# A two-layer hybrid block: two of layer 1's modulation products moved from its input projections to the start of the layer

## The chip, the cores and the metric

One Trainium2 chip, one core of it. The time is the device time of one execution in microseconds (us); lower is better.

## The reference

256 latent and 256 context tokens of width 1024 in float32 pass two layers. Cut to what matters here:

```python
for l in range(DEPTH):                                    # 2
    mod_l = split(silu(c) @ ada_w[l] + ada_b[l], 6)       # shift, scale, gate; shift, scale, gate
    mod_c = split(silu(c_ctx) @ ada_w[l] + ada_b[l], 6)
    pl = modulate(rms_norm(xl, norm1_g[l]), mod_l[0], mod_l[1]) @ w_in[l]
    pc = modulate(rms_norm(xc, norm1_g[l]), mod_c[0], mod_c[1]) @ w_in[l]
    ml, mc = token_mixing(pl, pc, ...)                    # pooling, two attentions, gated MLP
    xl = xl + mod_l[2] * (ml @ w_out[l])
    hl = modulate(rms_norm(xl, norm2_g[l]), mod_l[3], mod_l[4])
    xl = xl + mod_l[5] * grouped_moe(hl, ...)             # 16 experts, 2 for each token
    ...                                                   # the same for xc in layer 0
return rms_norm(xl, final_g)
```

The modulation (`c @ ada_w[l]`) depends on no token. `ada_w[l]` is 1024 x 6144, 24 MB for each layer.

## The kernel before, in words

The five engines run programs written out by hand, tied by semaphores; the order of instructions on each engine is that of the source.

**Weights in blocks.** Every large weight is loaded in blocks of 256 columns (1 MB; the second block of `w_in` is 160 columns, 0.64 MB) into a ring of six slots `raw`. All loads are issued by one queue, SP, in the order of `ORDER[l]` (line 354 on), and each waits until the block six places ahead of it has left its slot (`free_slot`, line 520; the load itself is line 548). A block of `w_in`, `w_out` or an expert is split on ACT and DVE into a rounded part `w_hi` and a rest `w_lo` (lines 808 and 1803; for experts 1033 and 2068), and TensorE (PE) takes three products for each (lines 1176 to 1178, for one kind of block 1298 to 1300). A block of `ada_w` is not split: PE multiplies it as it is.

**Modulation in quads.** A quad is four blocks of `ada_w`, one of the six vectors of a layer, quads 0 to 5 for layer 0 and 6 to 11 for layer 1. `modulate` (line 1197, the products are line 1205) waits until its four blocks have landed and runs 32 matmuls, four column groups by eight, into one PSUM bank. DVE copies the result to `mod_row` (`take_rows`, line 1824), PE transposes it (`turn`, line 1213), and DVE adds the bias and writes the vector (`take_modulation`, line 1832, with 1839 for the two scale vectors 7 and 10). `AFTER_BLOCK` names the block of `w_in` behind which a quad is computed; quads 6 and 7 of layer 1 are computed in layer 0, quads 9 and 10 in the projections of layer 1 behind its blocks 3 and 5, quads 8 and 11 in the attentions of the two layers (`IN_ATTENTION`). Quad 8 and the four before it are so all ready before layer 1 starts. Quads 9 and 10 are read first in the second half of layer 1.

**Between the layers.** The expert outputs of layer 0 are stored to DRAM. When the stores have landed, POOL gathers each token's two rows back, a 128-token tile at a time, eight gathers of 512 KB (line 773), and then clears a tile (line 672) on which SP's `small_loads` of layer 1 wait (line 560 on: seven small parameters, the last of them `na_bias`, two transfers in pieces of 256 bytes). For each tile ACT scales one row (line 862) and DVE adds the other (line 1890). Then `combine` works in eight units (four tiles by two halves): PE transposes four 128 x 128 pieces (line 1244), DVE adds them, gated, to the stream `x_t` (line 1897), ACT squares the result (line 856), PE sums the squares (line 1256). The eight sums end in a root on ACT, a reciprocal on DVE, and `rows_of` (line 1194) on PE, which spreads it. Then the norm of layer 1 delivers its input piece by piece, and PE starts block 0.

Meanwhile SP has put the first six blocks of layer 1 into the slots of the last experts (`next_layer`), then it sends the small loads, then it goes on with the order. ACT and DVE split blocks 0 and 1 ahead of the norm.

**Projections.** Eight blocks of `w_in` follow each other on PE (`W_COLS`); behind each come small products (`after_block`) and, where named, a quad, whose turn stands in the middle of the next block (`between`). From block 3 on each is split behind the block two before it (`SPLIT_AFTER`).

Of the kernel before, what the change touches and what calls it, by code (L numbers as in the profile page):

```python
# [115 lines left out]
def build(nc, a, out):  # L116
    with ExitStack() as ctx:  # L117
# [129 lines left out]
        assert M.at <= area_at + area_size  # L247

        mod_row = nc.alloc_sbuf_tensor_at("mod_row", [P, 2, BW], F32, offset=sgu_w_at)

        pair_hi = [xg_hi, nc.alloc_sbuf_tensor_at("pair_hi", [P, KC, 2 * SLOTS], F32R, offset=h_at + 2 * KC * T)]
        pair_lo = [xg_lo, nc.alloc_sbuf_tensor_at("pair_lo", [P, KC, 2 * SLOTS], F32R, offset=h_at + 6 * KC * T)]
# [81 lines left out]
        def rounds_before(l):  # L334
            return sum(ROUNDS[:l])
# [9 lines left out]
        W_COLS = [6, 7, 5, 4, 0, 1, 2, 3]  # L345
        W_SLOT = [0, 1, 2, 0, 1, 0, 1, 0]
        OUT_SLOT = [0, 1, 2, 1]
        AFTER_BLOCK = [{2: 2, 3: 3, 4: 4, 5: 5, 6: 6, 7: 7}, {3: 9, 5: 10}]
        IN_ATTENTION = [8, 11]
        SPLIT_AFTER = [{1: (3,)}, {1: (3,), 2: (4,), 3: (5,), 4: (6,), 5: (7,)}]  # L350
        SPLIT_FIRST = [{3: 4, 4: 5, 5: 6, 6: 7}, {}]
        ORDER = []
        for l in range(DEPTH):
            w_in_blocks = [(l, N_ADA + b) for b in range(N_WIN)]
            w_out_blocks = [(l, N_ADA + N_WIN + b) for b in range(N_WOUT)]
            order = quad(0) + quad(1) if l == 0 else []
            for n in range(N_WIN):
                order = order + [w_in_blocks[n]]
                if n in AFTER_BLOCK[l]:
                    order = order + quad(AFTER_BLOCK[l][n])  # L360
            ORDER.append(order + quad(IN_ATTENTION[l]) + w_out_blocks)

# [148 lines left out]
        def combine_units(l):  # L511

            return [(t, half) for t in range(2 * streams(l)) for half in range(2)]
# [659 lines left out]
        def _(pe):  # L1173
# [35 lines left out]
            def turn(q, dst):  # L1209

                pe.wait_ge(m_row, q + 1)
                for c in range(2):
                    ins = pe.transpose(dst[:, BW + c * P:BW + (c + 1) * P], mod_row[:, q % 2, c * P:(c + 1) * P], ident)
                ins.then_inc(m_turn, 1)

            def norm(i, width):

                n = width // P
                if i == 0:
                    for k in range(KC):  # L1220
                        pe.wait_ge(n_sqa if k % 2 == 0 else n_sqd, k // 2 + 1)
                        column_sums(bank[6], nsq[:, k % 4, :], k, n, k == KC - 1).then_inc(n_sum, 1)
                    turn(0, bank[START_BANK[0]])
                if i == 2 * DEPTH:
                    for c in range(KC):
                        pe.wait_ge(n_sqc, DEPTH * KC + c + 1)
                        column_sums(bank[SUM_BANK[i]], nsq_f[:, c % 4, :], c, n, c == KC - 1).then_inc(n_suc, 1)
                pe.wait_ge(n_rstd, i + 1)
                rows_of(bank[7], rstd, n).then_inc(n_bc, 1)
                if i == 0:  # L1230
                    modulate(1, bank[START_BANK[1]])
                    turn(1, bank[START_BANK[1]])

            def combine(l, u):

                units = combine_units(l)
                n = sum(len(combine_units(i)) for i in range(l))
                t, half = units[u]
                pe.wait_ge(q_c, n // 2 + t + 1)
                if u >= 3:  # L1240
                    pe.wait_ge(x_moe, n + u - 2)
                for c in range(4):
                    k = 4 * half + c
                    ins = pe.transpose(bank[4 + u % 3][:, c * P:(c + 1) * P], y_back[:, t, 0, k * P:(k + 1) * P], ident)
                ins.then_inc(q_ct, 1)
                if u >= 2:
                    unit_sums(l, u - 2)
                if u == len(units) - 1:
                    unit_sums(l, u - 1)
                    unit_sums(l, u)  # L1250
# [15 lines left out]
            for l in range(DEPTH):  # L1266
# [3 lines left out]
                if l == 0:  # L1270
                    pe.wait_ge(s_xin, 64)
                    for k in range(KC):
                        if k >= 6:
                            pe.wait_ge((s_xevd, s_xev)[k % 2], 1)
                        for t in range(4):
                            ins = pe.transpose(bank[X_BANK[k]][:, t * P:(t + 1) * P], x_tok[t][:, k * P:(k + 1) * P], ident)
                        ins.then_inc(s_xt, 1)
                    modulate(0, bank[START_BANK[0]])
                else:

                    pe.wait_ge(q_ya, E * rounds_before(l))
                    pe.wait_ge(q_yd, E * rounds_before(l))
                    for u in range(len(combine_units(l - 1))):
                        combine(l - 1, u)
                norm(2 * l, T)


                def by_feature(n, dst, c0, m, width, l=l):
                    s = W_SLOT[n]
                    for k in range(KC):  # L1290
                        ins = product(dst[0:m, 0:width], w_hi[s][:, k, c0:c0 + m], w_lo[s][:, k, c0:c0 + m],
                                      h_hi[:, k, 0:width], h_lo[:, k, 0:width], k == 0, k == KC - 1)
                    return ins
# [72 lines left out]
                for n in range(N_WIN):  # L1366
                    wait_split(l, N_ADA + n)
                    if n >= 2:
                        pe.wait_ge(proj_ea, l * 6 + (1, 2, 3, 4, 4, 5)[n - 2])
                        pe.wait_ge(proj_ed, l * 5 + (1, 2, 2, 2, 3, 3)[n - 2])  # L1370
                    b0 = 2 * (n % 2)

                    def between(n=n):
                        if n - 1 in AFTER_BLOCK[l]:
                            turn(AFTER_BLOCK[l][n - 1], bank[7])

                    if n == 0:
                        s = W_SLOT[0]
                        for k in range(KC):
                            pe.wait_ge(n_lo, l * KC + k + 1)  # L1380
                            for c in range(2):
                                cs = slice(c * P, (c + 1) * P)
                                ins = product(bank[c][:, 0:width], w_hi[s][:, k, cs], w_lo[s][:, k, cs],
                                              h_hi[:, k, 0:width], h_lo[:, k, 0:width], k == 0, k == KC - 1)
                    elif n == 1:
                        by_feature(n, bank[2], 0, P, T)
                        ins = by_feature(n, bank[3], P, 2 * ROPE, T)
                    elif W_COLS[n] in (3, 4, 5):
                        for t in range(4 if W_COLS[n] == 3 else nt):
                            if t == 1:  # L1390
                                between()
                            ins = by_token(n, bank[b0 + t // 2][:, (t % 2) * BW:(t % 2 + 1) * BW], t)
                    else:
                        for c in range(2):
                            if c == 1:
                                between()
                            ins = by_feature(n, bank[b0 + c], c * P, P, T if W_COLS[n] == 2 else width)
                    ins.then_inc(used, 1)
                    if n in AFTER_BLOCK[l]:
                        q = AFTER_BLOCK[l][n]  # L1400
                        if q > min(AFTER_BLOCK[l].values()):
                            pe.wait_ge(s_mod, q)
                        modulate(q, bank[7])
                    after_block(n)
# [383 lines left out]
        def _(dve):  # L1788
# [30 lines left out]
            def take_rows(q, src):  # L1819

                dve.wait_ge(ada_mm, q + 1)
                if q >= 2:
                    dve.wait_ge(m_turn, q - 1)
                dve.tensor_copy(mod_row[:, q % 2, :], src[:, 0:BW]).then_inc(m_row, 1)

            def take_modulation(q, src):

# [74 lines left out]
            for l in range(DEPTH):  # L1902
                ns = streams(l)
                nt, width = 2 * ns, ns * S
                if l == 0:
                    for k in range(0, KC, 2):
                        dve.wait_ge(s_xt, k + 1)
                        dve.tensor_copy(x_t[:, k, :], bank[X_BANK[k]][:, :]).then_inc(s_xevd, 1)
                    dve.wait_ge(s_xev, 4)
                else:  # L1910
                    for r in range(HL - 1):
                        split(l, N_ADA + r)
                    for u in range(len(combine_units(l - 1)) + 1):
                        combine(l - 1, u)
                    dve.wait_ge(x_moe, sum(len(combine_units(n)) for n in range(l)))

                def before_modulation():
# [2 lines left out]
                    take_rows(1, bank[START_BANK[1]])  # L1920
                    take_modulation(1, bank[START_BANK[1]])

                norm(2 * l, T, False, None if l else before_modulation)
                if l == 0:
                    split(0, N_ADA + 1)
                split(l, N_ADA + HL - 1)
# [448 lines left out]
```

## Time and profile before

| | |
|---|---|
| median of 3 runs | 933.02 us (931.19 to 935.28) |
| profiled execution, its own time | 933.12 us |
| its span, first to last instruction | 931.3 us |
| mean granted PE clock | 0.935 |
| PE busy | 841.8 us, 90% |
| DVE busy | 552.3 us, 59% |
| ACT busy | 463.6 us, 50% |
| POOL busy | 78.3 us, 8% |
| DMA | 197.49 MB, 212 GB/s over the span |

Busy is the time in which an engine had an instruction in work, as a share of the span; overlapping matmuls count once. The granted clock is 1.00 at 2.4 GHz and 0.50 at 1.2 GHz. Times in the views are us from the start of the span. A row of the timeline is one instruction or several alike, with start, length, engine and line, what is written from what, and their number; in brackets stands the time for which the engine had nothing to do before, and what ended it. SPq is the queue engine SP, whose rows are DMA issues; "to landing" is the time from an issue to the semaphore that tells its end.

### The profile page before, as it was taken

The page shows a single profiled execution, that of the slowest core. Times are in us where ns is not written, and L with a number is a line of the kernel's source. Part 1 is how long each engine was busy: PE and PEld are TensorE (multiplying, and loading weights), DVE is VectorE, ACT ScalarE, POOL GpSimd, SP SyncE. Part 2 cuts the span into 40 slices and gives each one's busy share as a digit, 9 for nine tenths or more (in the row PEclk, how much of TensorE's full clock was granted, in tenths as well). Part 3 has the DMA queues.
Part 4 walks back from the last instruction along what each step waited for, and adds up shares of the span by engine and source line. Part 5 has one row for each costly group of instructions (what it writes and reads, how often), then busy time and mean ns, then how long its engine had stood idle before and what let it go on. Part 6 is the DMA issues. An engine that isn't in the chain of part 4 may idle for free. (4 is left out here: it accounts for less than half of the span.)

```text
span 931.3 us, 15158 instructions
## 1 busy us (share of the span) xinstructions
PE 841.8 (90%) x6042; PEld 717.3 (77%) x6042; DVE 552.3 (59%) x804; ACT 463.6 (50%) x637; POOL 78.3 (8%) x103
## 2 busy tenths in 40 slices
PE   2899999899998889999999557999999799999986
PEld 2668866766787789999999456887769599999974
DVE  1363312359534878777777465444385678888953
ACT  1363112068523666655665336422384557776734
POOL 0102001600012000000000132001301100000000
PEclk9799999999998599999999856999999799999996
DMA  9795897793021158888888792269163249999901
GB/s 324 239 307 150 279 321 248 227 343 97 29 91 46 42 172 277 291 297 279 292 287 280 252 267 85 79 220 320 40 203 125 72 136 321 346 341 329 349 34 46
DMA packets 165442, 197.49 MB, mean 212 GB/s; under 512 B 11346, under 2 KB 152572, under 8 KB 165372
## 3 DMA queue, kind: packets, MB, share of 16 engines
q1 hardware_dynamic: 160720, 180.70, 60.7%
q10 hardware_dynamic: 3500, 11.64, 3.2%
q0 software_dynamic: 1152, 4.19, 1.4%
q8 instruction: 46, 0.75, 0.3%
q14 instruction: 24, 0.20, 0.1%
HBM read 187.09 MB, written 9.44 MB: 211 GB/s over the span
## 5 line engine op out<-in xcount | busy, mean ns | idle before, releaser
L2068 DVE TENSOR_TENSOR w_lo<-raw,w_hi 128x2048 fp32r<-128x2048 f32 x96 | 219.4, 2290 | 37.6 <-ACT w_hi L1033 37.0
L1033 ACT ACTIVATE w_hi<-raw 128x2048 fp32r<-128x2048 f32 x96 | 183.5, 1913 | 64.8 <-PE bank L1178 55.8
L1176 PE MATMUL bank<-h_hi,w_hi 128*128 128x512 f32 (+2 forms) x288 | 105.4, 366 | 12.0 <-DVE h_lo L1860 10.1
L1176 PE MATMUL bank<-w_hi,xg_hi 128*128 128x256 f32 x384 | 111.1, 289 | 2.3 <-DVE xg_lo L2229 1.7
L1177 PE MATMUL bank<-w_lo,xg_hi 128*128 128x256 f32 x384 | 108.6, 283 | 0.0
L1178 PE MATMUL bank<-w_hi,xg_lo 128*128 128x256 f32 x384 | 108.6, 283 | 0.0
L1177 PE MATMUL bank<-h_lo,w_hi 128*128 128x512 f32 (+2 forms) x288 | 101.6, 353 | 0.0
L1178 PE MATMUL bank<-h_hi,w_lo 128*128 128x512 f32 (+2 forms) x288 | 101.5, 353 | 0.0
L1803 DVE TENSOR_TENSOR w_lo<-raw,w_hi 128x2048 fp32r<-128x2048 f32 (+1 forms) x20 | 45.4, 2277 | 54.1 <-ACT w_hi L808 54.0
L808 ACT ACTIVATE w_hi<-raw 128x2048 fp32r<-128x2048 f32 (+1 forms) x20 | 37.2, 1866 | 76.9 <-PE bank L1178 26.2
L1176 PEld LDWEIGHTS bank<-w_hi,xg_hi 128*128 128x128 f32 x384 | 73.4, 191 | 2.7 <-issue 2.6
L1177 PEld LDWEIGHTS bank<-w_lo,xg_hi 128*128 128x128 f32 x384 | 73.6, 192 | 0.0
L1178 PEld LDWEIGHTS bank<-w_hi,xg_lo 128*128 128x128 f32 x384 | 73.5, 191 | 0.0
L1176 PEld LDWEIGHTS bank<-h_hi,w_hi 128*128 128x128 f32 (+1 forms) x288 | 54.7, 190 | 23.5 <-issue 9.5
L1592 PE MATMUL bank<-onehot,h_tok 128*128 128x256 f32 x512 | 65.1, 286 | 1.3 <-DVE onehot L2074 1.3
L1592 PEld LDWEIGHTS bank<-onehot,h_tok 128*128 128x128 f32 x512 | 64.1, 194 | 2.3 <-ACT h_tok L880 1.7
L1178 PEld LDWEIGHTS bank<-h_hi,w_lo 128*128 128x128 f32 (+1 forms) x288 | 54.8, 190 | 8.2
L1177 PEld LDWEIGHTS bank<-h_lo,w_hi 128*128 128x128 f32 (+1 forms) x288 | 54.9, 191 | 7.7 <-issue 0.2
L1176 PE MATMUL bank<-w_hi,ht_hi 128*128 128x512 f32 x128 | 51.9, 405 | 5.2 <-DVEq L2332 2.6
L1178 PE MATMUL bank<-w_hi,ht_lo 128*128 128x512 f32 x128 | 51.3, 401 | 0.0
L1177 PE MATMUL bank<-w_lo,ht_hi 128*128 128x512 f32 x128 | 51.2, 400 | 0.0
L1205 PE MATMUL bank<-raw,c_pad 128*32 128x256 f32 x768 | 45.4, 390 | 1.3 <-DMA raw<-in_ada_w 1.3
(291 smaller groups left out, 1615.6 us busy)
## 6 DMA issues: line engine op xcount, KB each, us to landing
raw<-in_ada_w SPq DMA_DIRECT2D x48, 1024.0 KB, 10.2
raw<-in_moe_w_gate SPq DMA_DIRECT2D x32, 1024.0 KB, 6.0
raw<-in_moe_w_up SPq DMA_DIRECT2D x32, 1024.0 KB, 6.3
raw<-in_moe_w_down SPq DMA_DIRECT2D x32, 1024.0 KB, 5.0
raw<-in_w_in SPq DMA_DIRECT2D x14, 1024.0 KB, 10.5
raw<-in_w_out SPq DMA_DIRECT2D x8, 1024.0 KB, 9.1
y_rows<-y_sb ACTq DMA_DIRECT2D x16, 512.0 KB, 4.8
na_bias<-in_na_rpb SPq DMA_DIRECT2D x4, 384.0 KB, 8.7
```

The lines of the kernel that those rows point to most:

```text
L808: act.activation(w_hi[slot][:, :, 0:w], raw[n % RAW][:, :, 0:w], ACT.Copy).then_inc(split_hi, 1)
L1033: act.activation(w_hi[slot][:, :, :], raw[q][:, :, :], ACT.Copy).then_inc(split_hi, 1)
L1176: pe.matmul(dst, w_hi_, x_hi_, start=first, stop=False)
L1177: pe.matmul(dst, w_hi_, x_lo_, start=False, stop=False)
L1178: return pe.matmul(dst, w_lo_, x_hi_, start=False, stop=last)
L1205: ins = pe.matmul(dst[32 * g:32 * g + 32, 0:BW], c_pad[:, k, :], raw[raw_index(l, j) % RAW][:, k, :], start=(k == 0), stop=(k == KC - 1))
L1592: ins = pe.matmul(bank[c // 2][:, (c % 2) * 2 * SLOTS:(c % 2 + 1) * 2 * SLOTS], h_tok[part][:, t, c * P:(c + 1) * P], onehot[:, t, :], sta ...
L1803: dve.tensor_tensor(w_lo[slot][:, :, 0:w], raw[n % RAW][:, :, 0:w], w_hi[slot][:, :, 0:w].bitcast(F32), ALU.subtract).then_inc(split_lo, 1)
L2068: dve.tensor_tensor(w_lo[slot][:, :, :], raw[q][:, :, :], w_hi[slot][:, :, :].bitcast(F32), ALU.subtract).then_inc(split_lo, 1)
```

## The change

Quads 9 and 10 leave the projections. Quad 9 is computed on PE between the last expert of layer 0 and `combine`; its copy and its additions on DVE stand behind the two splits and ahead of the gathered tiles. Quad 10 is computed behind unit 3 of `combine`, that is when tiles 0 and 1 are through; its copy stands on DVE behind the last unit, its turn on PE behind the last sum, its additions between the reciprocal and the norm. Both use banks 2 and 3 and a row buffer of their own, `gap_row`, as the place of `mod_row` is taken by a small parameter there. PE's product of block 1, which writes bank 3, now waits for quad 10's additions. In the order of loads, all eight quad blocks stand behind block 1 of `w_in`, so that the six slots filled at the end of layer 0 hold blocks 0 and 1 and quad 9; quad 10, blocks 2 to 7 and quad 11 follow. No product and no load is added or taken away.

```diff
--- before.py
+++ after.py
@@ -247,6 +247,7 @@
         assert M.at <= area_at + area_size
 
         mod_row = nc.alloc_sbuf_tensor_at("mod_row", [P, 2, BW], F32, offset=sgu_w_at)
+        gap_row = nc.alloc_sbuf_tensor_at("gap_row", [P, 2, BW], F32, offset=area_at + 16384)
 
         pair_hi = [xg_hi, nc.alloc_sbuf_tensor_at("pair_hi", [P, KC, 2 * SLOTS], F32R, offset=h_at + 2 * KC * T)]
         pair_lo = [xg_lo, nc.alloc_sbuf_tensor_at("pair_lo", [P, KC, 2 * SLOTS], F32R, offset=h_at + 6 * KC * T)]
@@ -345,8 +346,9 @@
         W_COLS = [6, 7, 5, 4, 0, 1, 2, 3]
         W_SLOT = [0, 1, 2, 0, 1, 0, 1, 0]
         OUT_SLOT = [0, 1, 2, 1]
-        AFTER_BLOCK = [{2: 2, 3: 3, 4: 4, 5: 5, 6: 6, 7: 7}, {3: 9, 5: 10}]
+        AFTER_BLOCK = [{2: 2, 3: 3, 4: 4, 5: 5, 6: 6, 7: 7}, {}]
         IN_ATTENTION = [8, 11]
+        IN_GAP, GAP_BANK = [9, 10], [2, 3]
         SPLIT_AFTER = [{1: (3,)}, {1: (3,), 2: (4,), 3: (5,), 4: (6,), 5: (7,)}]
         SPLIT_FIRST = [{3: 4, 4: 5, 5: 6, 6: 7}, {}]
         ORDER = []
@@ -356,6 +358,8 @@
             order = quad(0) + quad(1) if l == 0 else []
             for n in range(N_WIN):
                 order = order + [w_in_blocks[n]]
+                if l == 1 and n == 1:
+                    order = order + quad(IN_GAP[0]) + quad(IN_GAP[1])
                 if n in AFTER_BLOCK[l]:
                     order = order + quad(AFTER_BLOCK[l][n])
             ORDER.append(order + quad(IN_ATTENTION[l]) + w_out_blocks)
@@ -1209,8 +1213,9 @@
             def turn(q, dst):
 
                 pe.wait_ge(m_row, q + 1)
+                rows = gap_row if q in IN_GAP else mod_row
                 for c in range(2):
-                    ins = pe.transpose(dst[:, BW + c * P:BW + (c + 1) * P], mod_row[:, q % 2, c * P:(c + 1) * P], ident)
+                    ins = pe.transpose(dst[:, BW + c * P:BW + (c + 1) * P], rows[:, q % 2, c * P:(c + 1) * P], ident)
                 ins.then_inc(m_turn, 1)
 
             def norm(i, width):
@@ -1280,8 +1285,13 @@
 
                     pe.wait_ge(q_ya, E * rounds_before(l))
                     pe.wait_ge(q_yd, E * rounds_before(l))
+                    modulate(IN_GAP[0], bank[GAP_BANK[0]])
+                    turn(IN_GAP[0], bank[GAP_BANK[0]])
                     for u in range(len(combine_units(l - 1))):
                         combine(l - 1, u)
+                        if u == 3:
+                            modulate(IN_GAP[1], bank[GAP_BANK[1]])
+                    turn(IN_GAP[1], bank[GAP_BANK[1]])
                 norm(2 * l, T)
 
 
@@ -1383,6 +1393,8 @@
                                 ins = product(bank[c][:, 0:width], w_hi[s][:, k, cs], w_lo[s][:, k, cs],
                                               h_hi[:, k, 0:width], h_lo[:, k, 0:width], k == 0, k == KC - 1)
                     elif n == 1:
+                        if l:
+                            pe.wait_ge(s_mod, IN_GAP[1] + 1)
                         by_feature(n, bank[2], 0, P, T)
                         ins = by_feature(n, bank[3], P, 2 * ROPE, T)
                     elif W_COLS[n] in (3, 4, 5):
@@ -1821,7 +1833,8 @@
                 dve.wait_ge(ada_mm, q + 1)
                 if q >= 2:
                     dve.wait_ge(m_turn, q - 1)
-                dve.tensor_copy(mod_row[:, q % 2, :], src[:, 0:BW]).then_inc(m_row, 1)
+                rows = gap_row if q in IN_GAP else mod_row
+                dve.tensor_copy(rows[:, q % 2, :], src[:, 0:BW]).then_inc(m_row, 1)
 
             def take_modulation(q, src):
 
@@ -1910,8 +1923,11 @@
                 else:
                     for r in range(HL - 1):
                         split(l, N_ADA + r)
+                    take_rows(IN_GAP[0], bank[GAP_BANK[0]])
+                    take_modulation(IN_GAP[0], bank[GAP_BANK[0]])
                     for u in range(len(combine_units(l - 1)) + 1):
                         combine(l - 1, u)
+                    take_rows(IN_GAP[1], bank[GAP_BANK[1]])
                     dve.wait_ge(x_moe, sum(len(combine_units(n)) for n in range(l)))
 
                 def before_modulation():
@@ -1920,7 +1936,10 @@
                     take_rows(1, bank[START_BANK[1]])
                     take_modulation(1, bank[START_BANK[1]])
 
-                norm(2 * l, T, False, None if l else before_modulation)
+                def gap_modulation():
+                    take_modulation(IN_GAP[1], bank[GAP_BANK[1]])
+
+                norm(2 * l, T, False, gap_modulation if l else before_modulation)
                 if l == 0:
                     split(0, N_ADA + 1)
                 split(l, N_ADA + HL - 1)
```

On PE between the layers, before (`y_back` is the gathered tile, `nsq_t` the squares, `rstd` the reciprocal root):

```order
L1244 MATMUL bank<-const,y_back 128x128 x12
L1256 MATMUL bank<-const,nsq_t 128x1 x4
L1244 MATMUL bank<-const,y_back 128x128 x4
...
L1244 MATMUL bank<-const,y_back 128x128 x4
L1256 MATMUL bank<-const,nsq_t 128x1 x12
L1194 MATMUL bank<-const,rstd 128x128 x4
```

and with the change, from behind the last product of quad 9 (`raw` times `c_pad` is a quad's product, 32 such rows; `gap_row` is its copied row):

```order
L1218 MATMUL bank<-const,gap_row 128x128 x2
L1249 MATMUL bank<-const,y_back 128x128 x12
L1261 MATMUL bank<-const,nsq_t 128x1 x4
L1249 MATMUL bank<-const,y_back 128x128 x4
L1261 MATMUL bank<-const,nsq_t 128x1 x4
...
L1249 MATMUL bank<-const,y_back 128x128 x4
L1261 MATMUL bank<-const,nsq_t 128x1 x4
...
L1249 MATMUL bank<-const,y_back 128x128 x4
L1261 MATMUL bank<-const,nsq_t 128x1 x12
L1218 MATMUL bank<-const,gap_row 128x128 x2
L1198 MATMUL bank<-const,rstd 128x128 x4
```

The 32 products of quad 10 stand between the units, and two turns have come, ahead of the first unit and ahead of the spreading.

On SP, before, from the last small parameter on:

```order
L573 DMA na_bias<-in_na_rpb 64x24x64 x2
L548 DMA raw_52<-in_ada_w 128x8x256 [waits split_lo,split_hi]
L548 DMA raw_53<-in_ada_w 128x8x256 [waits split_lo,split_hi]
L548 DMA raw_54<-in_w_in 128x8x256 [waits split_lo,split_hi]
L548 DMA raw_55<-in_w_in 128x8x256 [waits split_lo,split_hi]
L548 DMA raw_56<-in_ada_w 128x8x256 [waits ada_mm]
L548 DMA raw_57<-in_ada_w 128x8x256 [waits ada_mm]
```

and with the change:

```order
L577 DMA na_bias<-in_na_rpb 64x24x64 x2
L552 DMA raw_52<-in_ada_w 128x8x256 [waits split_lo,split_hi]
L552 DMA raw_53<-in_ada_w 128x8x256 [waits split_lo,split_hi]
L552 DMA raw_54<-in_ada_w 128x8x256 [waits ada_mm]
L552 DMA raw_55<-in_ada_w 128x8x256 [waits ada_mm]
L552 DMA raw_56<-in_w_in 128x8x256 [waits ada_mm]
L552 DMA raw_57<-in_w_in 128x8x256 [waits ada_mm]
```

In both orders the first two loads behind `na_bias` wait for the splits of blocks 0 and 1. The four blocks of quad 10 are now these two and the next two, which wait for quad 9's products (`ada_mm`), and so do blocks 2 and 3; blocks 4 to 7 wait for quad 10's products.

## Rows read from the trace of the kernel before

**Rows 1.** Table of stretches; after "us": busy us (instructions) per engine, clock, DMA, GB/s
```profile
520.00:522.00 2.00, 1.29 (x7) 0.82 (x5) 1.48 (x1) 1.36 (x3) 0.00 (x0) 1.00 1.05 389
...
530.00:540.00 10.00, 0.00 (x0) 0.00 (x0) 3.96 (x2) 3.28 (x2) 5.50 (x4) 0.50 0.41 119
...
560.00:562.00 2.00, 2.00 (x12) 2.00 (x11) 0.67 (x4) 0.63 (x1) 1.58 (x3) 0.50 1.10 349
...
570.00:580.00 10.00, 6.54 (x30) 5.60 (x30) 7.08 (x12) 9.69 (x18) 0.00 (x0) 0.63 0.00 0
```

**Rows 2.** Timeline of PE between the layers: start us, us, engine, line, operation [idle before]
```profile
543.90 1.94 PE L1244 MATMUL bank<-const,y_back 128*128 128x128 f32 x8 [17.01 <-DVE y_back L1890]
...
553.22 1.09 PE L1244 MATMUL bank<-const,y_back 128*128 128x128 f32 x4
...
561.47 5.12 PE L1256 MATMUL bank<-const,nsq_t 128*128 128x1 f32 x24
567.23 2.08 PE L1194 MATMUL bank<-const,rstd 128*128 128x128 f32 x8 [0.64 <-DVE rstd L1853]
572.74 0.55 PE L1176 MATMUL bank<-h_hi,w_hi 128*128 128x256 f32 x1 [3.44 <-DVE h_lo L1860]
```

**Rows 3.** Timeline of POOL and of the SP queue between the layers
```profile
545.81 0.33 POOL L672 MEMSET pool_bd<- 128x256 f32 x1
...
546.22 1.33 SPq L564 DMA_DIRECT2D pool_bd<-in_pool_w  x2
...
553.87 4.13 SPq L548 DMA_DIRECT2D raw<-in_ada_w  x2
```

**Rows 4.** Line 548, SP's block loads, in four stretches: start; time to landing
```profile
L548 SPq DMA_DIRECT2D raw<-in_ada_w x2: 368/368/368, 517.7 to 522.9; - x2
DMA to landing us min/median/max: 6.9/6.9/7.0
...
L548 SPq DMA_DIRECT2D raw<-in_ada_w x1: 1530/1530/1530, 556.5 to 556.5; - x1
DMA to landing us min/median/max: 10.8/10.8/10.8
...
L548 SPq DMA_DIRECT2D raw<-in_ada_w x2: 368/472/575, 613.5 to 613.9; - x2
DMA to landing us min/median/max: 5.3/6.6/7.8
...
L548 SPq DMA_DIRECT2D raw<-in_ada_w x1: 2827/2827/2827, 615.8 to 615.8; - x1
DMA to landing us min/median/max: 13.2/13.2/13.2
```

**Rows 5.** Timelines of PE and ACT in the projections of layer 1
```profile
609.80 3.66 PE L1205 MATMUL bank<-raw,c_pad 128*32 128x256 f32 x64
...
618.22 0.44 PE L1213 MATMUL bank<-const,mod_row 128*128 128x128 f32 x2 [0.36 <-DVE mod_row L1824]
...
636.25 0.50 PE L1176 MATMUL bank<-h_hi,w_hi 128*128 128x512 f32 x1 [0.87 <-DVE w_lo L1803]
...
631.96 1.91 ACT L808 ACTIVATE w_hi<-raw 128x2048 fp32r<-128x2048 f32 x1 [7.43 <-DMA raw<-in_w_in]
```

**Rows 6.** Layer 0's second quad: timeline of PE, table of stretches (columns as rows 1)
```profile
38.40 5.14 PE L1205 MATMUL bank<-raw,c_pad 128*32 128x256 f32 x64
...
38.40:41.40 3.00, 3.00 (x31) 1.39 (x34) 0.69 (x1) 1.91 (x1) 0.99 (x3) 0.50 0.25 77
...
43.60:48.20 4.60, 0.44 (x2) 0.20 (x2) 2.70 (x8) 3.51 (x6) 0.00 (x0) 1.00 0.75 222
```

**Rows 7.** Timeline of DVE between the layers
```profile
534.80 3.96 DVE L1803 TENSOR_TENSOR w_lo<-raw,w_hi 128x2048 fp32r<-128x2048 f32 x2 [7.17 <-ACT w_hi L808]
...
555.39 1.28 DVE L1890 SCALAR_TENSOR_TENSOR y_back<-y_back,pick 128x1024 f32<-128x1024 f32 x1
...
561.71 1.13 DVE L1897 SCALAR_TENSOR_TENSOR x_t<-bank,mod,x_t 128x128 f32<-128x128 f32 x4 [1.33 <-PE bank L1244]
```

## The prediction

> **What bounds the kernel now.** I read the page first, for the level: TensorE (PE) is busy 90% of the span, VectorE (DVE) 59% (the table above), and the slices have one long hole between the two layers. One core runs, so no slower core is to be looked for. Then the table of stretches: from 530 to 540 us PE has nothing to do and its granted clock is 0.50, that is 1.2 GHz; from 570 to 580 the 16 DMA engines move 0 GB/s while PE, DVE and ScalarE (ACT) work [rows 1]. From 584 us on, in the projections of layer 1, PE waits for something twice, 0.36 and 0.87 us [rows 5]. So the two places differ in kind: between the layers a chain of small steps sets the pace; in the projections PE itself is the bound, and each instruction taken from it comes off the end.
>
> The timeline of the gap shows the chain. PE starts at 543.90 after 17.01 us of waiting for the gathered rows. Then the units (a token tile's half) are transposed and their squares summed in steps of about 2.45 us: unit 4 at 553.22, the last sums to 561.47 + 5.12 = 566.6; the reciprocal roots are spread at 567.23, and the first product of layer 1 starts at 572.74 [rows 2]. PE runs at 1.2 GHz all that time (0.50 at 530, still 0.50 at 560, a mean of 0.63 from 570 to 580) [rows 1].
>
> The SP queue sets what can be loaded when. Its last issue for the old layer's slots is at 522.9 [rows 4]; then it waits for a POOL memset at 545.81, which stands on POOL behind the eight gathers; then it sends the small parameters, and only at 553.87 the next two blocks of 1 MB [rows 3]. The second of them is issued at 556.5 and lands 10.8 us later, at 567.3 [rows 4].
>
> **What goes from the projections: 8.9 us off the end.** Quads 9 and 10 (32 matmuls each, 64 rows in the trace) take 3.66 us each at full clock, less an overlap of 0.07 with what follows: 2 x 3.59 = 7.2 [rows 5]. The turn of quad 9 holds the products up by 0.7 (0.36 of waiting for the copied row, then the turn), that of quad 10, which waits for nothing, by 0.1. The wait of 0.87 at 636.25 goes too: ACT had waited 7.43 us for block 6, which stood on SP behind the quad's blocks, so its split came late [rows 5]. In the new order block 6 is asked for once quad 10 is computed, more than 30 us before its use. Sum 7.2 + 0.7 + 0.1 + 0.87 = 8.9; bounds 7.2 (turns and wait come back in another form) and 9.5. I find nothing that is late next there: with the blocks in place a split needs 1.91 us on ACT [rows 5] and half of 3.96 on DVE [rows 7], under PE blocks of 6 us and more. From block 6 on SP's order is the same.
>
> **Quad 9 behind the last expert: 0.** Its four blocks take the slots that blocks 2 and 3 and two of its own took. The last is issued at 522.9 and lands 6.9 to 7.0 us on, at 529.8 [rows 4]; the products need 5.1 to 7.3 us (below), so they end by 537, and PE's cover lasts to 543.90. DVE copies the row once the two splits are done (534.80 + 3.96 = 538.8 [rows 7]); the copy, the turn and the additions are 2 us more, before the first gathered tile is ready. Without that cover, the 5.1 us and the turn would stand in the chain. SP loses nothing: the memset at 545.81 holds it either way.
>
> **Quad 10 between the tiles: here is the bill.** PE reaches it after unit 3, at 553.2, where unit 4 starts now. Its first two blocks are issued at 553.87 as now; the third and fourth need only quad 9, long done, and follow in the same queue. When does the fourth land? The first two carry the small parameters' load with them and land by 567.3 [rows 4]. In the burst of 613.5 the second block landed at 613.9 + 7.8 = 621.7 and the fourth at 615.8 + 13.2 = 629.0, 7.3 us later [rows 4]: 574.6. By the rate of 349 GB/s at 560 to 562 us [rows 1] two blocks of 1.05 MB need 6.0 us: 573.3. I take 574, a wait of 20.8 us. Low bound: at 389 GB/s (520 to 522 us [rows 1]) they need 5.4 and nothing queues, 572.0 with 0.7 off for the first two; high bound 576, with blocks 2 and 3 right behind taking a share.
>
> The Trainium skill (DMA: Bandwidth & Descriptors, Anatomy of one DMA) fits a transfer as 2.0 us plus its bytes at 436 GB/s. By it four blocks in a train from 553.87 would land at about 565.5, an estimate, and the sum would end 8.5 us lower. The burst at 613.5 took 15.5 us for the same four blocks where the rule says 11.6, so the trace doesn't agree, and I go by the burst.
>
> Then the products themselves. They start after a long wait, at clock 0.50. The same 32 matmuls at 38.40 in layer 0 also began at 0.50 and took 5.14 us, as the clock rose to 1.00 on the way [rows 6]. I take 5.1; bounds are 3.66, all at 2.4 GHz, and twice that, 7.3. Everything waits behind them: DVE for the transposes of unit 4, ACT for DVE's results to square, the norm for the sums.
>
> From the transposes of unit 4 to the first product it takes 572.74 - 553.22 = 19.5 us now, PE bound at 1.2 GHz [rows 2]. Behind quad 10 the clock is up: in layer 0 it stayed at 1.00 for the 4.6 us after the quad though PE had 0.44 us of work [rows 6]. PE's steps of 2.45 then halve and DVE leads: four evictions of 1.13 and one addition of 1.28 [rows 7], 5.8 and with handovers 6.7 to the last eviction, where 9.6 pass now (562.84), and the sums no longer lag. I put the gain at 4.0; bounds 0 and 5.5. The turn of quad 10 and its four small DVE operations, about 1 us, stand beside the spreading of 2.08 us [rows 2]: 0, at most 0.5.
>
> So the first product comes at 574.0 + 5.1 + 19.5 - 4.0 = 594.6 instead of 572.7, 21.9 later, and the kernel ends 21.9 - 8.9 = 13.0 later. The profiled execution took 933.12 us (span 931.3), 0.1 above the median of 933.02 of the three runs shown. Forecast: 933.0 + 13.0 = **946.0 us**. The change fills the idle DMA time at 570 to 580, but it wants the data before that time begins.
>
> **Rivals.** (a) The clock doesn't rise under quad 10: 574 + 7.3 + 19.5 = 600.8, +28.1 - 8.9 = +19.2, 952.2 us. For it: the transposes and sums keep PE busy for 20 us now without a rise; against it: layer 0's quad [rows 6]. (b) The four blocks come in one dense train at the best rate seen, 4 x 2.7 us at 389 GB/s: 564.7, and the sum is 9.3 lower, +3.7, 936.7 us. For it: 520 to 522 us; against it: two blocks alone took until 567.3. The page's rule above is nearly this case. (c) The other side: quad 10's blocks are there when PE asks. The wait is gone and the change is worth 5.1 - 4.0 - 8.9 = -7.8, 925.2 us. It decides at the landing of the fourth block: the sum is zero at 553.2 + 7.8 = 561.0. The place is SP's queue behind the POOL memset; the new order moves nothing there, and 553.87 to 561.0 leaves 7.1 us for four blocks where the shortest landing of one is 5.3 [rows 4]. (d) The change does less than it says: the projections wait for a split or the small weights where the quads stood, and the wait in the gap is short, so that both halves come to nothing, +/-0. Against it: only two short waits there now.
>
> **How the numbers follow.** The forecast has 0.70, (a) 0.13, (b) 0.07, (c) 0.05, (d) 0.05. With its own bounds the forecast goes from 572.0 + 5.1 + 14.0 = 591.1, +18.4 - 9.0 = +9.4 (942.4), to 576 + 5.1 + 19.5 = 600.6, +27.9 - 8.9 = +19.0 (952.0). The range, 939 to 953, holds that, (a) and a little of the way to (b). About 0.5% (4.7 us) is what a measurement of this kernel can tell from no change. Faster by more: 0.05, from (c). Within it: (d) and half of (b), 0.08. Slower by more: 0.87.
>
> **What would show it.** In the changed profile: PE idle for some 20 us in front of the second group of quad products, released by a DMA of modulation weights, from about 553 to 574; the first group between 529 and 538 with nothing waiting for it; the first product of the layer at 592 to 597; after it no quad products before the attention and no wait for a split; the clock at 1.00 for some us after the second group. The forecast is wrong if that wait is under 15 us, if unit 4's transposes start before 575, or if the projections, from the first product to the attention's first scores, shrink by less than 7 us.

## The result, and the profile after

The changed kernel took 948.21 us (median of 4 runs, 947.7 to 948.75), the kernel before beside it 933.94 us (4 runs, 931.19 to 935.28): a ratio of 1.0157, 95% interval 1.0139 to 1.0175, or 14.3 us more. The profiled execution took 947.93 us, its span is 946.1 us, and its mean granted clock is 0.924, where 0.935 stood. The page of the changed kernel, its first lines:

```profile
span 946.1 us, 15159 instructions
...
PE 844.5 (89%) x6042; PEld 719.8 (76%) x6042; DVE 552.3 (58%) x804; ACT 463.7 (49%) x637; POOL 79.7 (8%) x103
```

PE's busy time rose by only 2.7 us, with the same products. Most of the time must lie in waits, and the timeline of PE between the layers has them (it answers to [rows 2]):

```profile
531.83 5.38 PE L1209 MATMUL bank<-raw,c_pad 128*32 128x256 f32 x64 [5.63 <-ACTq L1102]
...
543.09 1.97 PE L1249 MATMUL bank<-const,y_back 128*128 128x128 f32 x8 [4.23 <-DVE y_back L1903]
...
572.54 5.50 PE L1209 MATMUL bank<-raw,c_pad 128*32 128x256 f32 x64 [20.57 <-DMA raw<-in_ada_w]
577.98 0.66 PE L1249 MATMUL bank<-const,y_back 128*128 128x128 f32 x4
...
582.82 4.86 PE L1261 MATMUL bank<-const,nsq_t 128*128 128x1 f32 x24
588.31 2.07 PE L1198 MATMUL bank<-const,rstd 128*128 128x128 f32 x8
593.90 0.55 PE L1180 MATMUL bank<-h_hi,w_hi 128*128 128x256 f32 x1 [3.51 <-DVE h_lo L1873]
```

Quad 9 (531.83) lies under the wait for the gathers: the first transposes come at 543.09, not later than before. Quad 10 (572.54) lies under nothing: PE waits 20.57 us for its blocks, and DVE, which has to add what PE transposes, waits with it:

```profile
578.67 1.13 DVE L1910 SCALAR_TENSOR_TENSOR x_t<-bank,mod,x_t 128x128 f32<-128x128 f32 x4 [26.72 <-PE bank L1249]
...
580.91 3.24 DVE L1910 SCALAR_TENSOR_TENSOR x_t<-bank,mod,x_t 128x128 f32<-128x128 f32 x12
```

Why the blocks are late, by the SP queue in the same stretch (it answers to [rows 3]) and by the landings of its blocks, first the second and third, then the third and fourth (to [rows 4]):

```profile
545.49 1.33 SPq L568 DMA_DIRECT2D pool_bd<-in_pool_w  x2
...
549.20 4.66 SPq L577 DMA_DIRECT2D na_bias<-in_na_rpb  x2
553.96 9.48 SPq L552 DMA_DIRECT2D raw<-in_ada_w  x4
```

```profile
L552 SPq DMA_DIRECT2D raw<-in_ada_w x2: 1562/1866/2171, 556.7 to 558.3; - x2
...
DMA to landing us min/median/max: 9.7/10.3/11.0
...
L552 SPq DMA_DIRECT2D raw<-in_ada_w x2: 2171/2524/2877, 558.3 to 560.6; - x2
...
DMA to landing us min/median/max: 11.0/11.4/11.8
```

The queue is where it was: first block at 553.96. The fourth is issued at 560.6 and lands 11.8 us later, at 572.4; PE starts 0.1 us after. The table of stretches shows that PE and DVE did nothing meanwhile, while POOL worked for 6.4 us on small parameters, and what followed (columns as in [rows 1]):

```profile
553.00:572.00 19.00, 0.00 (x0) 0.00 (x0) 0.00 (x0) 0.65 (x1) 6.37 (x15) 0.50 1.13 292
...
578.00:581.00 3.00, 2.70 (x28) 2.62 (x24) 2.33 (x6) 0.63 (x1) 0.00 (x0) 1.00 0.56 134
...
586.00:594.00 8.00, 4.38 (x19) 3.72 (x19) 2.87 (x9) 3.07 (x7) 0.00 (x0) 0.50 0.79 253
```

The clock is at 1.00 behind the quad. It fell at about 583.2 us (1.00 in the stretch from 582 to 583, 0.58 from 583 to 584), and is at 0.50 while the last squares are summed and the norm is computed. In the projections, the table of waits of PE from 590 to 700 us has one row left; the waits for the quads' copies and for the late split ([rows 5]) are gone:

```profile
PE bank L1180 <- DVE h_lo L1873: 5.5, 4, 3.5
```

The span in three parts, cut at the first product of layer 1 and at the first scores of its attention (the starts of those rows of PE's timeline), for all profiles of this study; the last column is the length of the stretch at clock 0.50 around the router of layer 1:

| kernel | first product | from there to the scores | from the scores to the end | span | low clock |
|---|---|---|---|---|---|
| before | 572.74 | 91.41 | 267.15 | 931.3 | 13.7 |
| changed | 593.90 | 81.64 | 270.56 | 946.1 | 23.9 |
| e1, quad 9 alone | 572.71 | 85.69 | 267.3 | 925.7 | 13.7 |
| e2, quad 10 behind the last unit | 583.26 | 81.63 | 270.2 | 935.1 | 23.9 |
| e3, an eighth of quad 10 | 594.31 | 81.64 | 268.7 | 944.6 | 23.9 |
| e4, quad 10 in block 0 | 572.09 | 82.95 | 270.5 | 925.5 | 23.9 |
| e5, parameters behind | 585.69 | 81.66 | 267.4 | 934.8 | 13.7 |
| e6, blocks 2 and 3 ahead | 601.34 | 81.66 | 267.4 | 950.4 | 17.1 |
| e7, changed, again | 593.03 | 81.63 | 267.1 | 941.8 | 13.7 |
| e8, before, again | 573.47 | 91.44 | 267.5 | 932.4 | 13.7 |
| e9, e4 again | 574.41 | 82.96 | 270.2 | 927.6 | 23.9 |

For the change: +21.2 to the first product, -9.8 in the projections, and +3.4 in a part that the change doesn't touch: together +14.8, the difference of the two spans. The last column, 23.9 for 13.7, goes with the +3.4, and the last three experiments are about it.

### The profile page after: what moved, and what is told of

It reads as the page before. It is cut to its first block and busy times, and to the rows that moved or that the text cites. A ratio compares the mean times of both kernels' runs of the same rounds, so it can differ in the third digit from the quotient of the medians.

```text
span 946.1 us, 15159 instructions
## 1 busy us (share of the span) xinstructions
PE 844.5 (89%) x6042; PEld 719.8 (76%) x6042; DVE 552.3 (58%) x804; ACT 463.7 (49%) x637; POOL 79.7 (8%) x103
## 5 line engine op out<-in xcount | busy, mean ns | idle before, releaser
L1180 PE MATMUL bank<-h_hi,w_hi 128*128 128x512 f32 (+2 forms) x288 | 105.6, 366 | 10.5 <-DVE h_lo L1873 9.5
L1209 PE MATMUL bank<-raw,c_pad 128*32 128x256 f32 x768 | 47.9, 405 | 28.1 <-DMA raw<-in_ada_w 22.5
L1209 PEld LDWEIGHTS bank<-raw,c_pad 128*32 128x32 f32 x768 | 26.3, 117 | 47.1 <-issue 28.6
```

What stands on the lines that cost most here:

```text
L1180: pe.matmul(dst, w_hi_, x_hi_, start=first, stop=False)
L1209: ins = pe.matmul(dst[32 * g:32 * g + 32, 0:BW], c_pad[:, k, :], raw[raw_index(l, j) % RAW][:, k, :], start=(k == 0), stop=(k == KC - 1))
```

## The experiments

Each timed kernel is compared with the kernel before on the same chip: for e1 to e4 that took 933.81 us (25 runs, 931.3 to 939.21), for e5 and e6, on another chip, 934.09 us (13 runs).

**e1: quad 9 alone.** Is it the second quad that costs? Quad 10 goes back behind block 5, with its loads.

```diff
-        AFTER_BLOCK = [{2: 2, 3: 3, 4: 4, 5: 5, 6: 6, 7: 7}, {}]
+        AFTER_BLOCK = [{2: 2, 3: 3, 4: 4, 5: 5, 6: 6, 7: 7}, {5: 10}]
...
-        IN_GAP, GAP_BANK = [9, 10], [2, 3]
+        IN_GAP, GAP_BANK = [9], [2]
...
-                    order = order + quad(IN_GAP[0]) + quad(IN_GAP[1])
+                    order = order + quad(IN_GAP[0])
...
-                        if u == 3:
-                            modulate(IN_GAP[1], bank[GAP_BANK[1]])
-                    turn(IN_GAP[1], bank[GAP_BANK[1]])
...
```

> Only quad 9 stands between the layers; quad 10 is back behind block 5. My theory (the loss is one wait, for quad 10's third and fourth block, which are issued behind the small parameters): no wait of PE for a DMA in the gap, first product of layer 1 where it is before (within 0.5 us), the projections shorter by 3.7 + 0.9 (quad 9 and its turn) and by the 0.87 of the late split, since block 6 is no longer loaded behind a quad: 5.4 us faster than before, about 928 us. Rival (work put between the last expert and the gathered tiles delays them, through DVE or the weights' loads): first product later by 3 us or more, no faster than before.

Measured: 930.77 us (10 runs, 926.07 to 932.75), ratio 0.9958 (0.9935 to 0.9981), 3.0 us faster than before. PE's timeline:

```profile
532.60 5.89 PE L1209 MATMUL bank<-raw,c_pad 128*32 128x256 f32 x64 [5.28 <-ACTq L1102]
...
567.19 2.08 PE L1198 MATMUL bank<-const,rstd 128*128 128x128 f32 x8 [0.63 <-DVE rstd L1863]
572.71 0.55 PE L1180 MATMUL bank<-h_hi,w_hi 128*128 128x256 f32 x1 [3.44 <-DVE h_lo L1870]
```

The first product is where it was before the change ([rows 2]), so quad 9 costs nothing there, and the projections are 5.7 us shorter. The whole loss is quad 10's. The expectation of 5.4 us holds for the profile, which gained 5.6, and not for the medians, which gained 3.0; the ten executions spread over 6.7 us, and where the medians lost the 2.4 between is not shown.

**e2: quad 10 behind the last unit.** If the wait is a landing at a fixed time, work put ahead of it costs nothing.

```diff
-                        if u == 3:
+                        if u == 7:
                             modulate(IN_GAP[1], bank[GAP_BANK[1]])
```

> As the change, but quad 10 stands behind the last unit instead of behind unit 3. My theory: the fourth block lands at 572.5 as in the change and PE waits from about 567 only (5 to 6 us instead of 20.6); units 4 to 7 are through before. First product near 584.5 instead of 593.9, so about 9 us faster than the change, 939 us, still some 5 slower than before. Rival (the units and the quad disturb each other, or the transfers of the tiles are what is late): the first product stays within 3 us of the change's.

Measured: 938.79 us (10 runs, 935.86 to 941.5), ratio 1.0055 (1.0034 to 1.0076). PE's timeline:

```profile
560.10 5.12 PE L1261 MATMUL bank<-const,nsq_t 128*128 128x1 f32 x24
571.97 5.90 PE L1209 MATMUL bank<-raw,c_pad 128*32 128x256 f32 x64 [6.75 <-DMA raw<-in_ada_w]
...
583.26 0.44 PE L1180 MATMUL bank<-h_hi,w_hi 128*128 128x256 f32 x1 [3.51 <-DVE h_lo L1873]
```

The products start 0.6 us from where they did in the changed kernel, though PE's work ahead of them ended thirteen microseconds later (at 565.2 for 552.0): the landing sets the time. Behind it stand only the quad, the spreading and the norm, and of the 14.3 us 5.0 are left. By the table, the first product is 10.5 us later than before, since the blocks come at 572, when the first product could have started; the projections are 9.8 shorter; and the tail, from the scores to the end, is 3.1 longer. Without that tail the two kernels would be within 1 us of each other.

**e3: an eighth of quad 10.** The wait stays, but the products shrink from 32 matmuls to 4 (this leaves out seven eighths of quad 10's sum; the vector is the second scale of layer 1, not a shift, as the expectation has it). It asks what the products cost, and what they give back by the clock.

```diff
-            def modulate(q, dst):
+            def modulate(q, dst, steps=KC):
...
-                for k in range(KC):
+                for k in range(steps):
...
-                                        start=(k == 0), stop=(k == KC - 1))
+                                        start=(k == 0), stop=(k == steps - 1))
...
-                            modulate(IN_GAP[1], bank[GAP_BANK[1]])
+                            modulate(IN_GAP[1], bank[GAP_BANK[1]], 1)
```

> As the change, but quad 10 has 4 of its 32 matmuls (one of eight steps of the sum; the other seven are left out, so shift vector 4 of layer 1 lacks seven eighths of its sum). The wait for the four blocks is kept. My theory (the quad raises PE's clock, and the units behind it run faster for that): wait 20.6 as in the change, products 0.7 to 1 instead of 5.5, but the clock stays at 0.50 and the stretch from unit 4's transposes to the first product takes 19 to 19.5 us again instead of 15.9: about 1 us faster than the change, 947 us. Rival (the stretch is short because DVE and ACT had everything ready, whatever the clock): it stays at 16, and the time is 4.5 us under the change's, 943.7 us.

Measured: 945.19 us (944.25 to 946.44), ratio 1.0114 (1.0071 to 1.0157). PE's timeline, then the stretches:

```profile
573.69 1.08 PE L1209 MATMUL bank<-raw,c_pad 128*32 128x256 f32 x8 [20.76 <-DMA raw<-in_ada_w]
574.70 1.12 PE L1249 MATMUL bank<-const,y_back 128*128 128x128 f32 x4
...
594.31 0.55 PE L1180 MATMUL bank<-h_hi,w_hi 128*128 128x256 f32 x1 [3.51 <-DVE h_lo L1873]
```

```profile
576.00:590.00 14.00, 13.89 (x67) 13.49 (x67) 6.53 (x23) 4.07 (x6) 0.00 (x0) 0.50 1.06 335
```

Unit 4 starts 3.3 us earlier than in the changed kernel, and the first product comes 0.4 us later. From unit 4 on it took 594.31 - 574.70 = 19.6 us, the 19.5 of [rows 2], with the clock at 0.50; behind the whole quad it took 593.90 - 577.98 = 15.9. So the products cost 5.4 and gave back 3.7 through the clock, and nearly all of the loss is the wait. The time alone doesn't decide it: the median is 3.0 us under the change's, between the 1 of the theory and the 4.5 of the rival, and in the profile the tail is 1.9 us shorter than the change's. What decides is the 19.6 us at clock 0.50, which the rival put at 16.

**e4: quad 10 in block 0.** The blocks are there at 572, when block 0 begins. So the eight steps of the quad are put between the steps of block 0, where PE waits for the norm's pieces anyway, its turn between the two halves of block 1, and its additions ahead of DVE's wait of that block. The order of loads is the changed kernel's.

```diff
-        IN_GAP, GAP_BANK = [9, 10], [2, 3]
+        IN_GAP, GAP_BANK = [9, 10], [2, 4]
...
+                            if l and k and k < KC - 1:
+                                modulate_step(IN_GAP[1], bank[GAP_BANK[1]], k - 1)
+                                if k == KC - 2:
+                                    modulate_step(IN_GAP[1], bank[GAP_BANK[1]], k)
+                                    modulate_step(IN_GAP[1], bank[GAP_BANK[1]], k + 1)
                     elif n == 1:
...
                         by_feature(n, bank[2], 0, P, T)
+                        if l:
+                            turn(IN_GAP[1], bank[GAP_BANK[1]])
...
```

> Quad 9 as in the change; quad 10's 32 products stand in eight steps of four between the steps of block 0, which the norm paces (1.65 us a step, PE has about 0.7 to 1.3 us of work in it), its copy, turn and additions in block 1. My theory: the blocks land at about 572.5, when block 0 begins, so nothing waits; the steps fit into PE's idle time. First product where it is before, block 0 longer by 1 us at most, and the projections shorter by the 9.8 us that the change saved: 9 to 10 us faster than before, about 924 us. Rival (PE's time in block 0 is not free, at the low clock above all): block 0 grows by 3.7 us or more, 928 us.

Measured: 928.65 us (10 runs, 926.86 to 929.81), ratio 0.9945 (0.9927 to 0.9962): 5.2 us faster than before and 19.6 faster than the change, by the medians. PE's timeline and its waits:

```profile
572.09 0.55 PE L1180 MATMUL bank<-h_hi,w_hi 128*128 128x256 f32 x1 [3.44 <-DVE h_lo L1891]
...
575.22 1.08 PE L1220 MATMUL bank<-raw,c_pad 128*32 128x256 f32 x8
...
577.24 0.64 PE L1220 MATMUL bank<-raw,c_pad 128*32 128x256 f32 x8
...
583.15 1.50 PE L1220 MATMUL bank<-raw,c_pad 128*32 128x256 f32 x24
```

```profile
PE bank L1180 <- DVE h_lo L1891: 3.4, 1, 3.4
PE bank L1230 <- DVE gap_row L1855: 0.6, 1, 0.6
```

No wait of PE for a transfer is left (the second row is quad 9's turn), and while the norm delivers, PE computes the quad: of its waits for the norm's pieces (`h_lo`) one of 3.4 us is left. Block 0 takes 13.3 us where it took 12.3 (to the first product of block 1, at 585.40 and before at 584.99), the 1 us of the expectation and not the rival's 3.7. From the first product to the scores it takes 8.5 us less than before, of the 9.8 that the change gained, and at the scores e4 is 9.1 us ahead (655.04 for 664.15). The time was still 4.7 us over the expected 924, and near the rival's 928: in the profile the tail is 3.3 us longer than that of before (the fourth column of the table), which is most of the miss.

**e5: the parameters behind the quad.** The small loads, the last of them in pieces of 256 bytes, stand ahead of quad 10's blocks, and with them the wait for the memset.

```diff
-                    if p == (RAW if l else ORDER[0].index((0, N_ADA + 3))):
+                    if p == (RAW + 4 if l else ORDER[0].index((0, N_ADA + 3))):
                         small_loads(l)
```

> As the change, but SP's small loads of layer 1, with their wait for the POOL memset, stand behind quad 10's four loads instead of ahead of them. My theory (what counts is when the fourth block lands): the four are issued from about 537 to 545, as soon as blocks 0 and 1 are split, share the DMA engines with the gathered tiles (4.2 MB each, together 24 us at 350 GB/s from 536 on) and land near 560; the gathered tiles come some 2 to 6 us later. PE's wait falls from 20.6 to under 10, the first product to 580 to 584, 10 to 14 us faster than the change, 934 to 938 us. Rival (the wait is set by the number of bytes, not by the place in the queue, or the delayed tiles take all of it back): first product within 4 us of the change's 593.9.

Measured: 934.77 us (10 runs, 932.0 to 939.99), ratio 1.0017 (0.9994 to 1.0039). The block loads between 540 and 550 us, the gathers (line 777), and PE:

```profile
L552 SPq DMA_DIRECT2D raw<-in_ada_w x3: 368/5861/6978, 541.0 to 548.4; - x3
...
DMA to landing us min/median/max: 15.8/17.1/19.7
...
L777 POOL DMA_INDIRECT y_back<-y_rows,pick_row x8: 937/1060/2397, 534.9 to 546.7; - x8
...
DMA to landing us min/median/max: 8.8/9.1/9.3
```

```profile
551.78 1.11 PE L1249 MATMUL bank<-const,y_back 128*128 128x128 f32 x4 [5.40 <-DVE y_back L1903]
...
564.35 5.30 PE L1209 MATMUL bank<-raw,c_pad 128*32 128x256 f32 x64 [7.51 <-DMA raw<-in_ada_w]
...
585.69 0.55 PE L1180 MATMUL bank<-h_hi,w_hi 128*128 128x256 f32 x1 [3.52 <-DVE h_lo L1873]
```

The last block is issued twelve microseconds earlier but lands only 8.2 us earlier, as now the gathers and the blocks share the DMA engines: a gather's landing takes 9.1 us where it took 5.9 in the changed kernel, so that units 2 and 3 come later too. PE's wait is 7.5 us, under 10 as expected. The first product is 8.2 us earlier than in the change, but at 585.7 it misses the expected 580 to 584, since the last block landed at 564.2 and not near 560. The time of 934.8 was in the expected range all the same, with help: the profile's tail is 3.1 us shorter than the change's, which the expectation didn't count. So an earlier issue buys an earlier landing here, but only two thirds of it.

**e6: two blocks of the projection ahead of the quad.** If the quad's train is late by its place in the queue, 2 MB ahead of it make it later by their transfer.

```diff
-                    order = order + quad(IN_GAP[0]) + quad(IN_GAP[1])
+                    order = order + quad(IN_GAP[0])
+                if l == 1 and n == 3:
+                    order = order + quad(IN_GAP[1])
```

> As the change, but blocks 2 and 3 of the input weights are loaded ahead of quad 10 instead of behind it: the suspected wait is lengthened by two blocks and nothing else. My theory: each block is 3.0 to 3.2 us of transfer, the fourth block of quad 10 lands 6.0 to 6.4 later, at about 578.7, PE's wait grows to about 27, the first product to 600, the time to 954 us. Rival (the wait is for something other than bytes in this queue, as the gap's engines or a semaphore of layer 0): wait and time stay within 2 us of the change's.

Measured: 952.14 us (951.12 to 954.57), ratio 1.0192 (1.0169 to 1.0216). The SP queue, then PE:

```profile
555.97 3.82 SPq L554 DMA_DIRECT2D raw<-in_w_in  x2
559.84 11.18 SPq L554 DMA_DIRECT2D raw<-in_ada_w  x4
```

```profile
580.06 4.90 PE L1211 MATMUL bank<-raw,c_pad 128*32 128x256 f32 x64 [26.08 <-DMA raw<-in_ada_w]
```

The wait grew by 5.5 us and the first product came 7.4 us later, 2.0 of it because SP reached its first block that much later (555.97 for 553.96); the projections took 81.66 us as in the changed kernel. So the price follows the landing.

**e7, e8, e9: the changed kernel, the one before and e4 again.** They ask of the 3.4 us in the tail: chance of the clock, or the change's?

> The changed kernel once more, for its profile. In the first one 3.0 us of the 14.8 are lost where router and first expert of layer 1 run at clock 0.50 for 23.9 us instead of 13.7 (748.02 to 758 us in before). Theory A (chance: where the clock falls and rises differs from run to run): the stretch from the attention's first scores to the end is now 267 to 271 us, and differs from 270.6 by over 1 us in one of the three repeats. Theory B (the change itself shifts that stage so that the clock stays low): 270.6 again for this kernel and for quad 10 in block 0, 267.2 again for before.

> The kernel before once more, for its profile. Theory A (chance): attention's first scores to the end anywhere from 267 to 271 us, and not tied to the kernel. Theory B (tied to the kernel): 267.2 again with a low stretch of 13.7 us.

> The kernel with quad 10 in block 0 once more, for its profile. Theory A: 267 to 271 us from the attention's first scores to the end. Theory B: 270.5 again. In both: first product near 572, projections 82.9 us.

Measured, one execution each: 943.56, 934.21 and 929.42 us, beside 935.24 for the kernel before. The stretch in question is the one right ahead of the products of layer 1's first expert, where PE gathers that expert's tokens (line 1667 and after it 1685 of the kernel before), as the table of stretches shows it in the kernel before, in the changed one, and in the changed one again:

```profile
748.10:752.40 4.30, 3.77 (x34) 3.59 (x33) 2.50 (x8) 1.09 (x2) 0.00 (x0) 1.00 0.63 197
```

```profile
759.40:766.20 6.80, 6.80 (x33) 6.77 (x33) 2.42 (x7) 1.08 (x2) 0.00 (x0) 0.50 0.48 154
```

```profile
758.20:762.60 4.40, 3.87 (x35) 3.69 (x33) 2.92 (x8) 1.09 (x2) 0.00 (x0) 1.00 0.55 168
```

The same 33 or so matmuls kept PE busy for 6.80 us at 1.2 GHz in one execution of the changed kernel and for 3.87 at 2.4 GHz in the other. With the short stretch its tail is 267.1 us, the tail of before. So theory B fails for the changed kernel, and the change doesn't force the 3.4 us; for e8 and e9 both theories allow what came. The change's own part, with the short stretch on both sides, is 943.56 less 933.12 or less 934.21 (e8): 9.4 to 10.4 us, by single executions, and only e7 and e8 ran on one chip. Against the 935.24 of that chip, whose stretch isn't known, it would be 8.3. Whether the change makes the long stretch likelier stays open: its four timed runs, with mean clocks of 0.924 to 0.927 where e7 had 0.930, look like the long one, the kernel before had the short one twice in two profiles, and e4 the long one twice. e7 to e9 ran on a third chip.

## Why the prediction was right

The forecast was 946.0 us, 939 to 953; 948.21 was measured. By its own steps:

**Quad 9 at nothing.** It held: the first transposes at 543.09 for 543.90, and e1 shows it alone. One detail was wrong: PE did wait in front of it, 5.63 us, not for the blocks (the last was issued at 522.2 and landed 7.8 us later, at 530.0) but for a count that ACT's queue fills up at 531.8 (`q_ya`, line 1102), for the rounds of experts that aren't run. The forecast had no such wait; the cover took it.

**The landing.** I took 574 with bounds 572 to 576; it was 572.4, and the wait 20.57 for 20.8. Of the two models behind the 574, the rate was the better: the second block landed at 556.7 + 9.7 = 566.4 (forecast 567.3) and the fourth 6.0 us later, which is the 6.0 of 349 GB/s and not the 7.3 of the burst. The whole train took 572.4 - 553.96 = 18.4 us, where the burst took 15.5 for four blocks, so the forecast came near because it started from the landing of two blocks behind the small parameters, as the kernel before shows it. The Trainium skill (DMA: Bandwidth & Descriptors, Anatomy of one DMA), by which the train would have landed at about 565.5, an estimate, was 7 us too fast; its fit is for transfers on the gpsimd path, and these are issued by SP. Rival (b), at 564.7, was 8 us too fast. Rival (c), blocks there when PE asks, was off by eleven microseconds, its point of decision being 561.0. Rival (d) wanted a short wait in the gap and new waits in the projections, and neither came.

**The products.** 5.44 us (572.54 to 577.98) for 5.1. The rows of the same 32 matmuls last 4.90 us in e6, 5.30 in e5, 5.90 in e2 and 6.38 in e7, so this term moves by more than a microsecond from run to run.

**The clock.** The step from unit 4 to the first product was forecast at 19.5 - 4.0 = 15.5 and was 15.9; e3 shows the 3.7 us by taking the quad away. The parts of the gain were not as forecast. The last eviction ended 580.91 + 3.24 - 577.98 = 6.2 us behind unit 4's start, where 9.6 passed before and 6.7 were forecast, so 3.4 came from there and not 2.9. The sums still lagged, as the clock was down again at 583.2: from the last eviction to the first product it took 9.75 us for 9.90. The forecast had about 1.1 from sums that no longer lag. Rival (a) falls by the same row. Sum of the three: 572.54 + 5.44 + 15.92 = 593.90, forecast 594.6.

**The projections.** Forecast -8.9, measured -9.8. Nearly all of the 0.9 is in quad 10's term and in quad 9's turn, which were too small. Cutting both profiles at the same products, the quads' own time is 3.68 and 3.75 (forecast 3.59 each), quad 9's turn 0.89 (0.7), and quad 10's turn with the late split 1.42 (0.97).

**The sum.** With these terms the change costs 21.2 - 9.8 = 11.4 us, where 13.0 was forecast. The other 3.4 us of the profile go with the clock at the start of the experts. The forecast had no term for it, neither in its sum nor in its bounds; its range, made for other reasons, took it in. The two errors, 1.6 too much and 3.4 left out, offset each other in part, so the forecast looks better than its terms are, and that part is luck. The range itself was narrower than its own bounds: its upper corner kept the products at 5.1 and the projections at 8.9. With the 7.3 and 7.2 that the forecast had allowed for them, it would have been 576 + 7.3 + 19.5 - 572.7 - 7.2 = +22.9, 955.9 us, above the 953.

## What to carry to other kernels

Work that is to fill an idle stretch of an engine should have its data at the start of that stretch, not within it: read from the queue when its last block lands, and put the work behind that time. Here the same quad delayed the first product by 21 us at 553 us and by 10.5 at 565, and cost about 1.3 (e4's projections against the change's) among the products that start at 572, with one order of loads for all three. And when only one of two moved pieces has its cover, try each alone: e1 and e4 are both faster than either kernel given, 3.0 and 5.2 us under the time of before.

## What the runs showed of the hardware

Two executions of the changed kernel, with the same instructions, had the clock at 1.2 GHz for 13.7 and for 23.9 us around the router, and the tails behind it differed by 3.5 us; over all profiles the tail was 267.1 to 267.5 us with 13.7 or 17.1 and 268.7 to 270.6 with 23.9. Effects of 0.3% of this kernel can't be told from that by one profile.

Block loads put beside the gathers slowed both: in e5 an issue took up to 6.98 us on SP's queue where 0.37 is the least, a block of the quad landed 16 to 20 us after its issue where it took 9.4 to 11.8 in the changed kernel, and a gather 9.1 us for 5.9 (medians).
